# Where the last modulation blocks are accumulated, and when the first pair's second down weights are loaded

## The chip, the core and the metric

The kernel runs on one core of one Trainium2 chip. The metric is the device time of one execution in microseconds (us). The engines named below are TensorE (PE), VectorE (DVE), ScalarE (ACT), GpSimd (POOL) and SyncE (SP, which here only issues DMAs and waits).

## What is computed

One decoder layer on 512 tokens of width 1024, all in float32:

```python
ada = (silu(c) @ w_ada + b_ada).reshape(1, 6, 1024)      # six vectors
shift1, scale1, gate1, shift2, scale2, gate2 = ada
h = x * (1.0 + scale1) + shift1
q, k, v, cb, cc, cx = split(h @ w_in)                    # each 512 wide
attn = stick_breaking_attention(q, k, v)                 # 8 heads of 64
conv = cb * causal_depthwise_conv(cc * cx, conv_w)       # width 3
mix  = concatenate([attn, conv]) @ w_out
x  = layer_norm(ALPHA * x + gate1 * mix, ln1_g, ln1_b)
h2 = x * (1.0 + scale2) + shift2
moe = hierarchical_moe(h2)   # 32 experts, 2 of 8 in the best of 4 groups per token
x  = layer_norm(ALPHA * x + gate2 * moe, ln2_g, ln2_b)
```

Stick-breaking attention takes sigmoids of the scores, multiplies `1 - sigmoid` along the keys from behind (a scan), and multiplies that with the sigmoid of the score itself. An expert is `(silu(h @ w_gate) * (h @ w_up)) @ w_down`, with 3 x 1 MB of weights.

## The kernel before

Every engine's program is written out by hand, in one fixed order, with semaphores between the engines. SP carries nearly all the loads in one queue of instructions: a wait in it holds back all loads behind it.

**Stages.** (1) `shift1` and `scale1` and the first projections, as `x` and `w_in` arrive. (2) The rest of `w_in` in nine blocks of 1 MB (`w_stage`, two buffers) and the other four vectors of `ada` in sixteen blocks of 1 MB (`ada_stage`, three buffers, blocks 8 to 23). VectorE does a block in `ada(i)`: nine dependent instructions (lines 775, 777 seven times, 779) into `acc_rows`. Three buffers mean that the load of block i waits for `ada(i-3)`. (3) Four pairs of heads. (4) Output projection, norm, modulation, routing. (5) The experts, two at a time. (6) The second norm and the output.

**Stage 3, pair p.** PE (from line 1240 on) does `scores(p)` (line 1206), `attend(p-1)` (line 1237), and then `conv_proj(3p)`, `turn_probs(2p)`, `conv_proj(3p+1)`, `turn_probs(2p+1)`, `conv_proj(3p+2)`. `conv_proj(n)` (line 1226, eight matmuls) is one 128-column block of the convolution's three inputs, in the order cc, cc, cx, cx, cb, cb and the same again; it writes one PSUM bank and so waits until product n-1 has been read from it (`conv_ev`). `turn_probs(h)` (line 1215, ten transposes) waits for the probabilities of head h (`prob_done`). ScalarE takes the sigmoids, GpSimd masks them (lines 487 and 490), and VectorE does `weights_of(h)`: the scan (line 825) as soon as `stay` is masked, and the product (line 829) once `prob` is masked too. `conv(n)` on VectorE reads product n: nothing for cc (ScalarE copies it out), line 840 and three more instructions for cx, line 848 for cb. In pair 0 only `conv(2)` has work, in pair 1 `conv(3)`, `conv(4)` and `conv(5)`, in pair 2 `conv(8)`, in pair 3 `conv(9)`, `conv(10)` and `conv(11)`.

VectorE's loop over the pairs ends with what `ada_in_pair` lists: blocks 20 and 21 in pair 0, 22 in pair 1, 23 in pair 2, none in pair 3. Blocks 8 to 19 come before the loop.

**From stage 3 to 4.** SP waits for all of `ada` (line 368), then issues four small router loads (lines 369 to 372) and `wo`, the 4 MB of `w_out` (line 373), into space that `ada_stage` also used. PE does `attend(3)`, spreads rows 0 to 3 of `acc_rows` over the partitions (`spread_row`, line 1259), waits for `wo` (`ld_wo`) and starts `project_out(0)` (line 1273). `row_done` counts the spread rows: the rows 4 and 5 follow `project_out(0)`, the rows 6 and 7 come behind `route(2)`. ScalarE's queue issues the loads of `g1r` and `b1r`, 512 KB each (lines 654 and 655), behind the copy of `attend(3)`'s result.

**Expert weights.** A ring of three pairs, `w_gu[u][e]` and `w_dn[u][e]`: pair u, expert e, three 1 MB loads each. SP first waits for `row_done` 6. The space of `w_dn[0][1]` is the end of `acc_rows`, so its load (`load_dn(0, 1, HALF)`) also waits for `row_done` 8. Pair 1 waits for `av_done` 4 and `conv_ev` 12 (the end of stage 3), pair 2 for `out_done` 8 (all of the output projection), and its second expert for `logit_done` 4 and the stores of `h2`. From then on `refill` loads the next pair into what the last one freed: first the gate and up weights of pair 3 once `gu_done` is 1, that is once the first expert's matmuls (line 1347) are over. PE gets the first tokens by an indirect gather (`xg`, line 520), which waits for the slot table that VectorE and PE work out behind `route(3)`.

Of the kernel before, what the change touches and what calls it, by code (L numbers as in the profile page):

```python
# [46 lines left out]
HALF = NE // 2  # L47
# [45 lines left out]
def layer_kernel(nc, x, c, w_ada, b_ada, w_in, conv_w, w_out, ln1_g, ln1_b, w_router_group,  # L93
# [3 lines left out]
    with ctx:  # L97
# [6 lines left out]
        def sem(name):  # L104
            return ctx.enter_context(nc.semaphore(name))
# [148 lines left out]
        row_done, row_ev, rows_ready, scaled = sem("row_done"), sem("row_ev"), sem("rows_ready"), sem("scaled")  # L254
# [21 lines left out]
        def acc_of(i):  # L276
            return acc_rows[:, w_cols(i - ADA1)]
# [18 lines left out]
        def landed(eng, what):  # L296

            buf, ld, before_it = stage_of(what)
            eng.wait_ge(ld, 16 * (before_it + 1))
            return buf  # L300
# [23 lines left out]
        def _(sp):  # L324
# [31 lines left out]
            for what in SEQ:  # L356
                kind, i = what
# [17 lines left out]
            def load_gu(u, e, ex):  # L375
                for g, w in enumerate((w_gate, w_up)):
                    src = w[0, bass.ds(ex, 1)].rearrange("o (p k) f -> p (o k) f", k=KC)
                    sp.dma_start(w_gu[u][e][:, g], src).then_inc(ld_gu[u][e], 16)  # L378

            def load_dn(u, e, ex):  # L380
                src = w_down[0, bass.ds(ex, 1)].rearrange("o (a p) n -> p (o a) n", p=P)
                sp.dma_start(w_dn[u][e][:], src).then_inc(ld_dn[u][e], 16)  # L382
# [3 lines left out]
            for j in range(RING):  # L386
                if j == 1:
                    sp.wait_ge(av_done, NH // 2)
                    sp.wait_ge(conv_ev, len(CONV_OUT))
                if j == 2:  # L390
                    sp.wait_ge(out_done, 2 * TC)
                for e in range(2):
                    if (j, e) == (2, 1):
                        sp.wait_ge(logit_done, TC)
                        for n in range(2):
                            sp.wait_ge(st_h2[n], 32)
                    load_gu(j, e, j + e * HALF)
                    if (j, e) == (0, 1):
                        sp.wait_ge(row_done, 8)
                    load_dn(j, e, j + e * HALF)  # L400

            def refill(i, u, first=False):

# [346 lines left out]
        def _(dve):  # L750
# [3 lines left out]
            def did(ins):  # L754
                count[0] += 1
                ins.then_inc(dve_did, 1)

            def settle():

                dve.wait_ge(dve_did, count[0])  # L760

            def link(ins):
                did(ins)
                settle()
# [6 lines left out]
            def ada(i):  # L771

                st = landed(dve, ("ada", i))
                acc = acc_of(i)
                link(w.tensor_scalar(acc, st[:, 0], csil[:, 3, 0:1], None, ALU.mult))
                for k in range(1, KC):
                    link(w.scalar_tensor_tensor(out=acc, in0=st[:, k], scalar=csil[:, 3, k:k + 1], in1=acc,  # L777
                                                op0=ALU.mult, op1=ALU.add))
                w.scalar_tensor_tensor(out=acc, in0=b24[:], scalar=ident[:, i:i + 1], in1=acc,
                                       op0=ALU.mult, op1=ALU.add).then_inc(ada_done, 1)  # L780
# [35 lines left out]
            dve.wait_ge(consts, 1)  # L816
            for i in range(ADA1, 20):
                ada(i)
            ada_in_pair = {0: (20, 21), 1: (22,), 2: (23,), 3: ()}

            def weights_of(h):

                st = stay[h % 2]
                dve.wait_ge(stay_masked, 2 * h + 2)
                w.tensor_tensor_scan(out=st[:, 0:ZW][:, ::-1], data0=st[:, 0:ZW][:, ::-1], data1=block_end[:, ::-1],  # L825
                                     initial=1.0, op0=ALU.mult, op1=ALU.max).then_inc(scan_done, 1)
                dve.wait_ge(scan_done, h + 1)
                dve.wait_ge(take_masked, 2 * h + 2)
                w.tensor_tensor(prob[h % 2][:], prob[h % 2][:], st[:, 1:ZW + 1], ALU.mult).then_inc(prob_done, 1)

            def conv(n):
                kind, f = CONV_OUT[n]
                y, u = cc_sb[f % 2], u_conv
                if kind == "cc":
                    return
                dve.wait_ge(conv_done, n + 1)
                dve.wait_ge(conv_ev, n)
                settle()
                if kind == "cx":
                    w.tensor_tensor(u[:], ps[:, 6], y[:], ALU.mult).then_inc(conv_ev, 1)  # L840
                    dve.wait_ge(conv_ev, n + 1)
                    link(w.tensor_scalar(y[:], u[:], cwT[:, 2 * NF + f:2 * NF + f + 1], None, ALU.mult))
                    link(w.scalar_tensor_tensor(out=y[:, 1:], in0=u[:, :T - 1], scalar=cwT[:, NF + f:NF + f + 1],
                                                in1=y[:, 1:], op0=ALU.mult, op1=ALU.add))
                    did(w.scalar_tensor_tensor(out=y[:, 2:], in0=u[:, :T - 2], scalar=cwT[:, f:f + 1],
                                               in1=y[:, 2:], op0=ALU.mult, op1=ALU.add))
                else:
                    w.tensor_tensor(mixT[:, NF + f], ps[:, 6], y[:], ALU.mult).then_inc(conv_ev, 1)

            dve.wait_ge(consts, 8)  # L850
            for p in range(NPH):
                weights_of(2 * p)
                conv(3 * p)
                weights_of(2 * p + 1)
                conv(3 * p + 1)
                conv(3 * p + 2)
                for i in ada_in_pair[p]:
                    ada(i)


            dve.wait_ge(row_ev, 6)
# [249 lines left out]
            i = TC - 1  # L1111
# [341 lines left out]
```

## Time and profile before

| | us |
|---|---|
| median of 3 runs | 607.32 (606.79 to 608.8) |
| profiled execution, own time | 606.77 |
| profiled execution, span | 605.0 |
| PE busy | 492.3 (81%) |
| VectorE busy | 284.1 (47%) |
| DMA, over the span | 164.11 MB, mean 271 GB/s |

Times in the rows are counted from the span's start. Between the span and the execution's own time lie 1.8 us that no row shows. The page cuts the span into 40 slices of 15.1 us. Its chain of the work that ended last is PE to 54%, SP's queue to 15%, DMA to 12% and VectorE to 11% of the span. An entry such as "[4.93 <-DVE prob L829]" says that the engine stood idle for 4.93 us before that row, and that what ended the wait was line 829 on VectorE.

### The profile page before, as it was taken

How to read it: one execution, taken by the hardware profiler on the slowest of the kernel's cores; microseconds unless marked ns; L12 is line 12 of the kernel's file. 1: busy time of each engine (PE TensorE's matmuls, PEld its weight loads, DVE VectorE, ACT ScalarE, POOL GpSimd, SP SyncE). 2: the span in 40 equal slices, each digit the busy share in tenths (PEclk: the TensorE clock that was granted, in tenths of full speed). 3: DMA queues.
4: the chain of work that ended last, by engine and by line, in shares of the span. 5: the costliest groups of instructions: out<-in, count | busy, mean ns of one | idle time of the engine just before them, and what ended most of it. 6: DMA issues, size and time to landing. Idle time of an engine off the chain costs nothing.

```text
span 605.0 us, 6476 instructions
## 1 busy us (share of the span) xinstructions
PE 492.3 (81%) x2426; PEld 263.9 (44%) x2426; DVE 284.1 (47%) x481; ACT 99.8 (16%) x161; POOL 125.8 (21%) x117
## 2 busy tenths in 40 slices
PE   2999999996999999999813999999979778887100
PEld 1545478443544444445512555555534434444000
DVE  4566999529481920785376132232321121122395
ACT  1000210413141411011221111211111111010010
POOL 2000000603060400455542012111111111000076
PEclk9999999999999999999855999999998988899755
DMA  8998789505022341730199999999999999996433
GB/s 296 355 363 255 254 281 311 179 1 195 14 69 71 94 195 70 284 133 35 64 421 414 385 385 415 414 416 417 417 418 416 419 418 417 417 419 282 157 150 134
DMA packets 66723, 164.11 MB, mean 271 GB/s; under 512 B 7768, under 2 KB 43660, under 8 KB 58508
## 3 DMA queue, kind: packets, MB, share of 16 engines
q1 hardware_dynamic: 60992, 152.22, 66.0%
q0 software_dynamic: 4608, 8.40, 3.7%
q10 hardware_dynamic: 1100, 3.19, 1.3%
q8 instruction: 14, 0.23, 0.2%
q14 instruction: 9, 0.07, 0.0%
HBM read 159.59 MB, written 12.58 MB: 285 GB/s over the span
## 4 chain that ended last, share of the span: by engine, by line
PE 54%; SPq 15%; DMA 12%; DVE 11%; POOL 3%; issue 2%; ACT 1%; POOLq 1%; DVEq 0%
SPq L378 10%; PE ps L1226 10%; PE ps L1347 9%; DMA w_gu<-in_w_up_dram 8%; PE ps L1149 7%; PE ps L1273 7%; PE ps L1196 5%; SPq L382 4%; PE ps L1356 4%; PE ps L1189 2%; DVE acc_rows L777 2%; PE ps L1215 2%; PE ps L1259 1%; DMA xs<-in_x_dram 1%; PE ps L1340 1%
## 5 line engine op out<-in xcount | busy, mean ns | idle before, releaser
L1347 PE MATMUL ps<-w_gu,xT 128*64 128x256 f32 x1024 | 126.4, 403 | 24.8 <-DMA w_gu<-in_w_up_dram 21.7
L1347 PEld LDWEIGHTS ps<-w_gu,xT 128*64 128x64 f32 x1024 | 75.4, 144 | 66.3 <-DMA w_gu<-in_w_up_dram 17.2
L1226 PE MATMUL ps<-hT,w_stage 128*128 128x512 f32 x192 | 85.7, 600 | 0.0
L1049 DVE TENSOR_TENSOR hid<-ps,silu_sb 128x128 f32<-128x128 f32 x32 | 9.3, 292 | 127.7 <-ACT silu_sb L704 113.8
L1057 DVE TENSOR_TENSOR ysb<-ps,rows_gate 64x512 f32<-64x512 f32 x64 | 44.0, 688 | 51.9 <-PE ps L1356 51.4
L1356 PE MATMUL ps<-w_dn,hidT 128*64 128x512 f32 x256 | 61.3, 599 | 0.6 <-ACT hidT L698 0.4
L526 POOL DMA_INDIRECT y_dram<-ysb,slot_row x16 | 16.1, 1005 | 202.2 <-DVE ysb L1057 202.2
L777 DVE SCALAR_TENSOR_TENSOR acc_rows<-ada_stage,csil,acc_rows 128x256 f32<-128x256 f32 x112 | 55.3, 494 | 4.0
L1273 PE MATMUL ps<-wo,mixT 128*128 128x512 f32 x128 | 55.6, 592 | 0.0
L1226 PEld LDWEIGHTS ps<-hT,w_stage 128*128 128x128 f32 x192 | 36.0, 192 | 41.6 <-issue 41.6
L1149 PE MATMUL ps<-hT,w_first 128*128 128x512 f32 x96 | 45.1, 618 | 0.9 <-DVE hT L803 0.9
L1273 PEld LDWEIGHTS ps<-wo,mixT 128*128 128x128 f32 x128 | 24.2, 190 | 29.6 <-issue 29.6
L704 ACT ACTIVATE silu_sb<-ps 128x128 f32<-128x128 f32 x32 | 8.9, 277 | 139.7 <-PE ps L1347 136.4
L487 POOL TENSOR_SCALAR_AFFINE_SELECT stay<-stay 128x384 f32<-128x384 f32 x8 | 5.3, 660 | 127.7 <-ACT stay L618 127.7
L1196 PE MATMUL ps<-w_stage,hT 128*128 128x256 f32 x128 | 27.8, 379 | 0.0
L1356 PEld LDWEIGHTS ps<-w_dn,hidT 128*64 128x64 f32 x256 | 17.1, 136 | 24.0 <-issue 20.9
L1149 PEld LDWEIGHTS ps<-hT,w_first 128*128 128x128 f32 x96 | 18.3, 199 | 20.2 <-issue 20.2
L825 DVE TENSOR_TENSOR_SCAN stay<-stay,block_end 128x1280 f32<-128x1280 f32 x8 | 23.8, 2975 | 5.5 <-POOL stay L490 5.5
L1196 PEld LDWEIGHTS ps<-w_stage,hT 128*128 128x128 f32 x128 | 24.3, 190 | 3.7 <-issue 0.5
L1340 PE MATMUL ps<-ident,xg 128*128 128x128 f32 x128 | 18.4, 289 | 9.3 <-DMA xg<-h_dram,slot_tok 9.3
L789 DVE SCALAR_TENSOR_TENSOR acc_cols<-ada_in,csil,acc_cols 128x512 f32<-128x512 f32 x28 | 21.1, 752 | 1.2 <-DMA ada_in<-in_w_ada_dram 0.2
L1340 PEld LDWEIGHTS ps<-ident,xg 128*128 128x128 f32 x128 | 14.4, 146 | 15.2 <-DMA xg<-h_dram,slot_tok 9.4
(184 smaller groups left out, 479.2 us busy)
## 6 DMA issues: line engine op xcount, KB each, us to landing
w_gu<-in_w_gate_dram SPq DMA_DIRECT2D x32, 1024.0 KB, 19.2
w_gu<-in_w_up_dram SPq DMA_DIRECT2D x32, 1024.0 KB, 23.3
w_dn<-in_w_down_dram SPq DMA_DIRECT2D x32, 1024.0 KB, 24.5
ada_stage<-in_w_ada_dram SPq DMA_DIRECT2D x16, 1024.0 KB, 7.2
w_stage<-in_w_in_dram SPq DMA_DIRECT2D x9, 1024.0 KB, 9.6
ada_in<-in_w_ada_dram SPq DMA_DIRECT2D x16, 512.0 KB, 9.7
wo<-in_w_out_dram SPq DMA_DIRECT2D x1, 4096.0 KB, 14.4
y_tok<-y_dram SPq DMA_DIRECT2D x8, 512.0 KB, 7.4
```

The costliest lines, as they stand in the source:

```text
L378: sp.dma_start(w_gu[u][e][:, g], src).then_inc(ld_gu[u][e], 16)
L382: sp.dma_start(w_dn[u][e][:], src).then_inc(ld_dn[u][e], 16)
L777: link(w.scalar_tensor_tensor(out=acc, in0=st[:, k], scalar=csil[:, 3, k:k + 1], in1=acc, op0=ALU.mult, op1=ALU.add))
L825: w.tensor_tensor_scan(out=st[:, 0:ZW][:, ::-1], data0=st[:, 0:ZW][:, ::-1], data1=block_end[:, ::-1], initial=1.0, op0=ALU.mult, op1=ALU. ...
L1057: ins = w.tensor_tensor(ysb[u][e * HD:(e + 1) * HD, b * 512:(b + 1) * 512], ps[b * HD:(b + 1) * HD, 6 + e, :], gate2r[b * HD:(b + 1) * HD, ...
L1149: ins = t.matmul(ps[:, n], w_first[:, k, n * P:(n + 1) * P], hT[:, k], start=k == 0, stop=k == KC - 1)
L1196: ins = t.matmul(dst[:, 0:CW], hT[:, k, i * P:(i + 1) * P], st[:, k], start=k == 0, stop=k == KC - 1)
L1226: ins = t.matmul(ps[:, 6], st[:, k, (f % 2) * P:(f % 2 + 1) * P], hT[:, k], start=k == 0, stop=k == KC - 1)
L1273: ins = t.matmul(ps[:, 4 + 2 * (i % 2) + n], mixT[:, k, i * P:(i + 1) * P], wo[:, k, n * 512:(n + 1) * 512], start=k == 0, stop=k == KC - 1)
L1340: ins = t.transpose(flat[:, k * P:(k + 1) * P], xg[u][:, k * P:(k + 1) * P], ident[:])
L1347: ins = t.matmul(ps[a * SLOTS:(a + 1) * SLOTS, 2 + e, 0:2 * P], xT[u][:, k, e * SLOTS:(e + 1) * SLOTS], w_gu[slot][e][:, :, k, a * P:(a + ...
L1356: ins = t.matmul(ps[b * SLOTS:(b + 1) * SLOTS, 6 + e, :], hidT[e][:, a * SLOTS:(a + 1) * SLOTS], w_dn[slot][e][:, a, b * 512:(b + 1) * 512 ...
```

## The change

Two edits. On VectorE each pair now does one block of `ada`, 20 + p, right behind `weights_of(2p + 1)` and ahead of `conv(3p + 1)`. On SP the load of the first pair's second down weights, with its wait for `row_done` 8, moves from the end of pair 0 to behind pair 1 and the wait for `out_done`.

```diff
@@ SP @@
                 if j == 2:
                     sp.wait_ge(out_done, 2 * TC)
+                    sp.wait_ge(row_done, 8)
+                    load_dn(0, 1, HALF)
                 for e in range(2):
...
                     load_gu(j, e, j + e * HALF)
-                    if (j, e) == (0, 1):
-                        sp.wait_ge(row_done, 8)
-                    load_dn(j, e, j + e * HALF)
+                    if (j, e) != (0, 1):
+                        load_dn(j, e, j + e * HALF)
@@ VectorE @@
             for i in range(ADA1, 20):
                 ada(i)
-            ada_in_pair = {0: (20, 21), 1: (22,), 2: (23,), 3: ()}
...
                 weights_of(2 * p + 1)
+                ada(20 + p)
                 conv(3 * p + 1)
                 conv(3 * p + 2)
-                for i in ada_in_pair[p]:
-                    ada(i)
```

VectorE, the last pair, from the end of pair 2 on. Names: `stay` and `prob` with the head's buffer number, `cc_sb` the convolution's buffer, `ada_stage` the block, `ps` the PSUM. Before:

```order
L775 TENSOR_SCALAR acc_rows_66<-ada_stage0_63,csil_139 128x256
L777 SCALAR_TENSOR_TENSOR acc_rows_66<-ada_stage0_63,csil_139,acc_rows_66 128x256 x7
L779 SCALAR_TENSOR_TENSOR acc_rows_66<-b24_87,ident_121,acc_rows_66 128x256
L825 SCALAR_TENSOR_TENSOR stay0_68<-stay0_68,block_end_70 128x1280
L829 TENSOR_TENSOR prob0_89<-prob0_89,stay0_68 128x1280
L840 TENSOR_TENSOR u_conv_86<-ps,cc_sb1_92 128x512
L842 TENSOR_SCALAR cc_sb1_92<-u_conv_86,cwT_138 128x512
L843 SCALAR_TENSOR_TENSOR cc_sb1_92<-u_conv_86,cwT_138,cc_sb1_92 128x511
L845 SCALAR_TENSOR_TENSOR cc_sb1_92<-u_conv_86,cwT_138,cc_sb1_92 128x510
L825 SCALAR_TENSOR_TENSOR stay1_69<-stay1_69,block_end_70 128x1280
L829 TENSOR_TENSOR prob1_90<-prob1_90,stay1_69 128x1280
L848 TENSOR_TENSOR mixT_106<-ps,cc_sb0_91 128x512
```

And now, from the first scan of the last pair on:

```order
L825 SCALAR_TENSOR_TENSOR stay0_68<-stay0_68,block_end_70 128x1280
L829 TENSOR_TENSOR prob0_89<-prob0_89,stay0_68 128x1280
L840 TENSOR_TENSOR u_conv_86<-ps,cc_sb1_92 128x512
L842 TENSOR_SCALAR cc_sb1_92<-u_conv_86,cwT_138 128x512
L843 SCALAR_TENSOR_TENSOR cc_sb1_92<-u_conv_86,cwT_138,cc_sb1_92 128x511
L845 SCALAR_TENSOR_TENSOR cc_sb1_92<-u_conv_86,cwT_138,cc_sb1_92 128x510
L825 SCALAR_TENSOR_TENSOR stay1_69<-stay1_69,block_end_70 128x1280
L829 TENSOR_TENSOR prob1_90<-prob1_90,stay1_69 128x1280
L776 TENSOR_SCALAR acc_rows_66<-ada_stage0_63,csil_139 128x256
L778 SCALAR_TENSOR_TENSOR acc_rows_66<-ada_stage0_63,csil_139,acc_rows_66 128x256 x7
L780 SCALAR_TENSOR_TENSOR acc_rows_66<-b24_87,ident_121,acc_rows_66 128x256
L848 TENSOR_TENSOR mixT_106<-ps,cc_sb0_91 128x512
```

Block 23 (three rows with `acc_rows`) has gone from ahead of the last pair's first scan to between its last product and the first line 848; pair 1 has the same new order with block 21.

SP's queue, from the first pair's second expert to the third pair (`w_gu01` is pair 0, expert 1). Before:

```order
L378 DMA w_gu01_50<-in_w_gate_dram 128x2048
L378 DMA w_gu01_50<-in_w_up_dram 128x2048
L382 DMA w_dn01_56<-in_w_down_dram 128x2x1024 [waits row_done]
L378 DMA w_gu10_51<-in_w_gate_dram 128x2048 [waits conv_ev,av_done]
L378 DMA w_gu10_51<-in_w_up_dram 128x2048
L382 DMA w_dn10_57<-in_w_down_dram 128x2x1024
L378 DMA w_gu11_52<-in_w_gate_dram 128x2048
L378 DMA w_gu11_52<-in_w_up_dram 128x2048
L382 DMA w_dn11_58<-in_w_down_dram 128x2x1024
```

And now:

```order
L378 DMA w_gu01_50<-in_w_gate_dram 128x2048
L378 DMA w_gu01_50<-in_w_up_dram 128x2048
L378 DMA w_gu10_51<-in_w_gate_dram 128x2048 [waits conv_ev,av_done]
L378 DMA w_gu10_51<-in_w_up_dram 128x2048
L382 DMA w_dn10_57<-in_w_down_dram 128x2x1024
L378 DMA w_gu11_52<-in_w_gate_dram 128x2048
L378 DMA w_gu11_52<-in_w_up_dram 128x2048
L382 DMA w_dn11_58<-in_w_down_dram 128x2x1024
L382 DMA w_dn01_56<-in_w_down_dram 128x2x1024 [waits row_done,out_done]
```

The load of `w_dn01`, with the wait for `row_done`, stands behind the six loads of pair 1.

## Rows read from the trace of the kernel before

**Rows 1.** Page, part 2: what the DMA engines moved, in 40 slices of 15.1 us.

```profile
GB/s 296 355 363 255 254 281 311 179 1 195 14 69 71 94 195 70 284 133 35 64 421 414 385 385 415 414 416 417 417 418 416 419 418 417 417 419 282 157 150 134
```

**Rows 2.** Chain that ended last, 296 to 345 us: start us, us, what.

```profile
319.86 7.50 DMA xg<-h_dram,slot_tok
```

**Rows 3.** Busy time by stretch: length, engines, PEclk, DMA share, GB/s.

```profile
151.00:152.00 1.00, 1.00 (x6) 1.00 (x5) 0.93 (x3) 0.00 (x0) 0.00 (x0) 0.50 0.62 197
335.00:338.00 3.00, 2.52 (x29) 1.47 (x27) 1.02 (x6) 0.54 (x2) 0.00 (x0) 1.00 0.83 269
```

**Rows 4.** PE in time, attention stage: start us, us, line, idle before and releaser.

```profile
138.00 7.13 PE L1226 MATMUL ps<-hT,w_stage 128*128 128x512 f32 x16
150.06 2.16 PE L1215 MATMUL ps<-ident,prob 128*128 128x128 f32 x10 [4.93 <-DVE prob L829]
152.02 7.91 PE L1226 MATMUL ps<-hT,w_stage 128*128 128x512 f32 x16
...
160.85 7.05 PE L1226 MATMUL ps<-hT,w_stage 128*128 128x512 f32 x16
...
207.85 1.31 PE L1215 MATMUL ps<-ident,prob 128*128 128x128 f32 x10 [0.57 <-DVE prob L829]
...
216.96 7.05 PE L1226 MATMUL ps<-hT,w_stage 128*128 128x512 f32 x16
...
229.78 13.90 PE L1273 MATMUL ps<-wo,mixT 128*128 128x512 f32 x32
```

**Rows 5.** VectorE in time, the same stage and the same columns.

```profile
97.95 0.35 DVE L775 TENSOR_SCALAR acc_rows<-ada_stage,csil 128x256 f32<-128x256 f32 x1
...
102.39 0.35 DVE L775 TENSOR_SCALAR acc_rows<-ada_stage,csil 128x256 f32<-128x256 f32 x1
...
112.01 2.82 DVE L825 TENSOR_TENSOR_SCAN stay<-stay,block_end 128x1280 f32<-128x1280 f32 x1 [5.10 <-POOL stay L490]
115.49 1.72 DVE L829 TENSOR_TENSOR prob<-prob,stay 128x1280 f32<-128x1280 f32 x1 [0.66 <-POOL prob L490]
...
133.45 0.69 DVE L840 TENSOR_TENSOR u_conv<-ps,cc_sb 128x512 f32<-128x512 f32 x1 [11.24 <-PE ps L1226]
...
149.93 0.68 DVE L840 TENSOR_TENSOR u_conv<-ps,cc_sb 128x512 f32<-128x512 f32 x1
...
152.62 2.82 DVE L825 TENSOR_TENSOR_SCAN stay<-stay,block_end 128x1280 f32<-128x1280 f32 x1
155.48 1.49 DVE L829 TENSOR_TENSOR prob<-prob,stay 128x1280 f32<-128x1280 f32 x1
```

**Rows 6.** GpSimd in time: the last mask of the third head's `stay`.

```profile
137.87 0.47 POOL L490 TENSOR_SCALAR_AFFINE_SELECT stay<-stay 128x128 f32<-128x128 f32 x1
```

**Rows 7.** PE in time, expert stage: two waits for weights.

```profile
454.15 5.34 PE L1347 MATMUL ps<-w_gu,xT 128*64 128x256 f32 x32 [2.79 <-DMA w_gu<-in_w_up_dram]
...
479.59 3.67 PE L1347 MATMUL ps<-w_gu,xT 128*64 128x256 f32 x32 [2.24 <-DMA w_gu<-in_w_up_dram]
```

**Rows 8.** SP queue in time: start us, us, issues.

```profile
203.24 0.55 SPq L369 DMA_DIRECT2D w_r<-in_w_router_group_dram  x1
...
205.72 0.43 SPq L373 DMA_DIRECT2D wo<-in_w_out_dram  x1
...
299.73 0.38 SPq L382 DMA_DIRECT2D w_dn<-in_w_down_dram  x1
```

**Rows 9.** ScalarE queue in time: first of the two norm loads.

```profile
226.37 0.35 ACTq L654 DMA_DIRECT2D g1r<-in_ln_g_dram  x1
```

**Rows 10.** DMA issues, KB each, median us to landing.

```profile
wo<-in_w_out_dram SPq DMA_DIRECT2D x1, 4096.0 KB, 14.4
...
g1r<-in_ln_g_dram ACTq DMA_DIRECT2D x1, 512.0 KB, 4.0
b1r<-in_ln_b_dram ACTq DMA_DIRECT2D x1, 512.0 KB, 5.0
```

**Rows 11.** Line 526 alone, window 562 to 566 us: landing time of the last scatter.

```profile
DMA to landing us min/median/max: 3.6/3.6/3.6
```

## The prediction

> **What bounds the kernel now.** I read the page's row of what the DMA engines moved first [rows 1]. From slice 20 to slice 35 (302 to 545 us) it stands at 385 to 421 GB/s and hardly moves: the expert stage is bound by its transfers. Before that (slices 16 to 19, 242 to 302 us) the engines are mostly idle, and PE sets the time, with gaps. So a microsecond won ahead of 302 us counts only as far as it brings the saturated stretch forward, and what brings that forward is to be read at its start.
>
> At that start the ring of six experts is being filled. SP has stood at the wait for `row_done` 8 until 299.73 us [rows 8], and then issues 13 loads of 1 MB, 13.6 MB, which at some 416 GB/s take 33 us, to about 335 us with their latency. The first refill can be issued when the first expert's gate and up matmuls are over, near 336 us. The stretch 335 to 338 us, the only dip there, still has the DMA engines 83% busy [rows 3]. The end of the filling and the first refill thus meet: neither hides much of the other. PE's start on the experts hangs on the gather of the first tokens: issued at 319.86 us, landed 7.50 us later, among those loads [rows 2].
>
> In the attention stage I look at PE in time for gaps [rows 4]: 4.93 us before 150.06 us, for a product of VectorE, and 0.57 us before 207.85 us, for another. VectorE shows why [rows 5]: it had blocks 20 and 21 to do ahead of pair 1's first scan, while earlier it had waited 11.24 us for PE ahead of 133.45 us. After the 4.93 us PE's clock is at 0.50 [rows 3], which is the lower level, 1.2 GHz.
>
> **Edit one, block by block.** A block takes 102.39 - 97.95 = 4.44 us [rows 5].
>
> Block 20 moves into the 11.24 us in which VectorE waited: nothing, as long as that cover is longer than 4.44 us.
>
> Block 21 leaves the front of pair 1. The mask of `stay` ends at 137.87 + 0.47 = 138.3 us [rows 6]. Scan and product, with GpSimd's masks between, take 115.49 + 1.72 - 112.01 = 5.2 us when nothing is ahead of them [rows 5], so the product is there at 143.6 us. PE ends `conv_proj(3)` at 138.00 + 7.13 = 145.1 us [rows 4] and no longer waits. Turning, projecting and turning again took 216.96 - 207.85 = 9.1 us at full clock and 160.85 - 150.06 = 10.8 us behind the gap, so 1.7 us of clock go too. PE is ready for `conv_proj(5)` at 154.2 us instead of 160.85: 6.6 us won.
>
> But that product needs its bank, and the bank is read by `conv(4)`, which now stands behind block 21. Line 840 starts at 145.2 us, its four instructions take 152.62 - 149.93 = 2.7 us, scan and product 155.48 + 1.49 - 152.62 = 4.35 us [rows 5]: 152.2 us. The block adds 4.44, the read 0.7: 157.4 us. So PE waits 3.2 us anew, behind ten short transposes, and 3.4 us of the 6.6 are left.
>
> Does the clock fall again there? Of two waits for weights in the expert stage, the one of 2.79 us is followed by matmuls that take 5.34 us, the one of 2.24 us by the same in 3.67 us [rows 7]. 3.2 us lies on the side of the fall, and the price is 5.34 - 3.67 = 1.7 us, the same as behind the 4.93. I take the fall: net 3.4 - 1.7 = 1.7 us won by the end of pair 1. The bounds are 0 and 1.7.
>
> Block 22 goes from pair 1's end into pair 2, ahead of `conv(8)`, where VectorE waits for PE as it did in pair 0: nothing. Block 23 leaves the front of pair 3, where PE waited 0.57 us [rows 4]; PE is there at 207.3 us less the 1.7. But it comes to stand ahead of `conv(10)`. From 207.3 us VectorE needs 2.7 + 4.35 + 4.44 = 11.5 us, to 218.8, less the 1.7: **block 23 ends at 217.1 us**, in the old order it ended ahead of 203.24 us, when SP went on [rows 8]. `conv(10)` ends at 217.8 us, while PE was ready at 207.3 + 9.1 - 1.7 = 214.7 us: 3.1 us of waiting, and likely 1.7 us of clock. PE has spread its rows at 229.78 - 216.96 + 217.8 + 1.7 = 232.3 us.
>
> What is queued behind block 23 is what costs. SP waits for it with five loads, `wo` the last. From the first to `wo` it took 205.72 - 203.24 = 2.5 us [rows 8], and `wo` lands 14.4 us after its issue [rows 10]: 217.1 + 2.5 + 14.4 = 234.0 us. Until now it landed at 220.1 us, 9.7 us ahead of its use, and that cover is gone. Moreover, ScalarE's two loads of 512 KB were issued at 226.37 us [rows 9], with `wo` long landed. Now they come near 229 us, into its flow. Nothing in the trace shows those three together, so the bounds are 0 and 1.05 MB / 416 GB/s = 2.5 us. I take 2.5: the gather of [rows 2] among loads took 7.5 us, while a scatter of no more bytes in quiet took 3.6 us [rows 11], so transfers of different queues do share. `project_out(0)` starts at 236.5 instead of 229.78 us: **6.7 us later**. PE has waited 4.2 us then, so one more fall of the clock, 1.7 us (bounds 0 and 1.7): **8.4 us**.
>
> The Trainium skill ("DMA: Bandwidth & Descriptors", section on queues, rings and completion order) says that each DMA engine goes round the queues that have work, a packet at a time. By that rule the two norm loads take their full bytes out of `wo`'s flow, and the stretch is at its upper end, against this change; with an order by arrival it would be 0 and the sum 2.5 us smaller. The rows of gather and scatter speak for the rule, no row shows it for `wo`.
>
> Behind `project_out(0)` nothing on PE's and VectorE's way to routing changes, and there is no slack between them: rows 4 and 5, the norm and three more products follow one another. The 8.4 us arrive whole at the gather's issue.
>
> **Edit two.** SP issues the six loads of pair 1 directly behind pair 0, near 256 us, into engines that are idle. That is 6.3 MB, 15.1 us at 416 GB/s, off what is left at `row_done` 8. The remaining 7.3 MB take 17.6 us and have landed about when the gather is issued. This doesn't bring the end forward by 15 us, since the first refill must still wait for the first expert; the DMA engines stand idle in between. What it gives is a gather in quiet: 3.6 us in place of 7.5, **3.9 us** sooner, bounds 0 and 3.9. That passes on: gather, transposes, first expert, first refill, and then 26 experts at an unchanged rate. Nothing waits behind the moved `row_done` 8 that could have gone earlier, but for pair 2's first expert, which waited there before as well. The stores of `h2` (two of them) now run among loads; nobody waits for these two closely.
>
> For the gather, the same page's section on the anatomy of one DMA gives 2.0 us plus bytes / 436 GB/s, an estimate of 3.2 us for 512 KB in quiet. By that the sum would be 0.4 us smaller.
>
> **Sum.** +6.7 +1.7 -3.9 = +4.5 us. The profiled execution took 606.77 us, span and the 1.8 us around it, and would become 611.3; it lies 0.55 us under the median of three. The median would be 607.32 + 4.5 = **611.8 us**.
>
> **Rivals.**
> A. The clock holds through the 3.2 us of pair 1. All from there is 1.7 us earlier, block 23 too: 610.1 us. For it: the 2.24 us that cost nothing. Against: 2.79 us that did, and the transposes ahead of the wait.
> B. `wo` isn't stretched by the norm loads: 2.5 us less, 609.3 us. Against it speaks the gather's 7.5 us.
> C. More than one of these, say the clock holds both in pair 1 and ahead of `project_out(0)`: 3.4 us less, 608.4 us, no difference that can be told.
> D. Faster: the filling of the ring is the bound, not the gather. If the refills could follow the last filling load at once, the 6.3 MB loaded early would shorten the saturated stretch by 15.1 us, and with +8.4 the time would be 600.6 us. It decides if the first expert's matmuls are over when the 7.3 MB have landed, near 320 us on the old scale. That the gather is issued only at 319.86 us [rows 2] speaks against it.
> E. Edit two gives nothing: the gather takes its 7.5 us even so (its cost lies elsewhere, or the loads of pair 2 still run). Then 607.32 + 8.4 = 615.7 us.
>
> **How the numbers follow.** Forecast 0.44, A 0.22, B 0.08, C 0.13, D 0.07, E 0.06. A measurement of this kernel tells about 0.3%, 1.8 us, from no change. Slower by more: forecast, A, E and half of B, 0.76. Within: C and half of B, 0.17. Faster: D, 0.07. The range 607.3 to 613.9 leaves out D, E and the edges: C down to no loss at all, and the forecast with a wait or a clock stretch some 2 us larger.
>
> **What would show it.** Right: no wait ahead of pair 1's first turning; waits near 3 us for line 848 ahead of `conv_proj(5)` and `conv_proj(11)`; PE waiting some 4 us for the load of `wo`, landed 16 to 17 us after its issue; DMA moving over 380 GB/s for some 27 us from 256 us on; an idle hole in it ahead of the first refill; the first gather in under 4.5 us. Wrong: `wo` landed ahead of PE's need, which would take 6 to 8 us from the sum, or a saturated stretch that starts by more than 5 us sooner against the gather's issue.

## The result, and the profile after

| | median us | single runs |
|---|---|---|
| before | 607.06 | 606.59 to 608.8 |
| the change | 614.15 | 612.26 to 614.85 |

The ratio is 1.0107, with a 95% interval of 1.0076 to 1.0137: slower, by 7.1 us where 4.5 were forecast. The ratio times the 607.32 us of the forecast is 613.8 us, at the very end of the range 607.3 to 613.9; the raw median, 614.15, lies 0.25 us outside it. Run again on other chips, the same kernel gave 609.97 us beside 607.44 (ratio 1.0047, 1.0029 to 1.0065, 12 runs) and 610.53 beside 606.96 (1.0073, 1.0044 to 1.0101, 7 runs). The three profiled executions of it have spans of 612.5, 610.8 and 609.2 us, against 605.0 before.

Lines of `kernel.py` differ by one or two between the versions (`conv_proj` is 1226 before and 1225 here, `project_out` 1273 and 1272). PE in time (start us, us, line, idle before and releaser), the attention stage and what follows, of the changed kernel; it answers to [rows 4]:

```profile
138.96 7.13 PE L1225 MATMUL ps<-hT,w_stage 128*128 128x512 f32 x16
145.93 1.26 PE L1214 MATMUL ps<-ident,prob 128*128 128x128 f32 x10
...
158.36 8.80 PE L1225 MATMUL ps<-hT,w_stage 128*128 128x512 f32 x16 [3.19 <-DVE mixT L848]
...
218.80 7.10 PE L1225 MATMUL ps<-hT,w_stage 128*128 128x512 f32 x16 [3.19 <-DVE mixT L848]
...
238.97 16.57 PE L1272 MATMUL ps<-wo,mixT 128*128 128x512 f32 x32 [7.13 <-DMA wo<-in_w_out_dram]
255.38 1.88 PE L1258 MATMUL ps<-acc_rows,ones 128*128 128x512 f32 x4
...
335.59 1.97 PE L1339 MATMUL ps<-ident,xg 128*128 128x128 f32 x8 [5.60 <-DMA xg<-h_dram,slot_tok]
```

This execution is 1.0 us late before anything that the change moves: `scores(0)` starts at 108.24 us and not at 107.28. Take that off every time here. The 4.93 us ahead of 150.06 us [rows 4] are gone: `turn_probs(2)` starts at 145.93 us, right behind `conv_proj(3)`. Two new waits of 3.19 us stand for line 848, at 158.36 and at 218.80 us. The first is followed by a product of 8.80 us (clock lost), the second by one of 7.10 (none lost). Then PE waits 7.13 us for `wo`, and the first product of the output projection takes 16.57 us instead of 13.90 [rows 4].

VectorE in time shows who holds back line 848; it answers to [rows 5]:

```profile
151.69 1.49 DVE L829 TENSOR_TENSOR prob<-prob,stay 128x1280 f32<-128x1280 f32 x1
153.09 0.35 DVE L776 TENSOR_SCALAR acc_rows<-ada_stage,csil 128x256 f32<-128x256 f32 x1
...
157.53 0.68 DVE L848 TENSOR_TENSOR mixT<-ps,cc_sb 128x512 f32<-128x512 f32 x1
...
213.54 0.35 DVE L776 TENSOR_SCALAR acc_rows<-ada_stage,csil 128x256 f32<-128x256 f32 x1
...
217.97 0.68 DVE L848 TENSOR_TENSOR mixT<-ps,cc_sb 128x512 f32<-128x512 f32 x1
```

The probabilities' product (line 829) ends at 153.1 us; the block goes from 153.09 to 157.53 us, and only then is the bank read. In pair 3 the block runs from 213.54 to 217.97 us.

SP's queue and the DMA issues (KB each, median us to landing), which answer to [rows 8, 10]:

```profile
218.08 0.55 SPq L369 DMA_DIRECT2D w_r<-in_w_router_group_dram  x1
...
220.56 0.43 SPq L373 DMA_DIRECT2D wo<-in_w_out_dram  x1
...
344.58 0.33 SPq L378 DMA_DIRECT2D w_gu<-in_w_gate_dram  x1
```

```profile
wo<-in_w_out_dram SPq DMA_DIRECT2D x1, 4096.0 KB, 18.4
...
g1r<-in_ln_g_dram ACTq DMA_DIRECT2D x1, 512.0 KB, 7.9
b1r<-in_ln_b_dram ACTq DMA_DIRECT2D x1, 512.0 KB, 10.1
```

`wo` goes out at 220.56 us, 14.8 us later than before, and takes 18.4 us and not 14.4; the two norm loads take twice as long as before. The first refill goes out at 344.58 us, 8.3 us later than before:

```profile
336.25 0.33 SPq L378 DMA_DIRECT2D w_gu<-in_w_gate_dram  x1
```

The chain of waits (start us, us, what) has the first gather, as in [rows 2], and the page's row answers to [rows 1] (slices of 15.3 us here):

```profile
331.74 3.81 DMA xg<-h_dram,slot_tok
```

```profile
GB/s 296 355 362 236 253 273 318 173 137 70 2 67 70 1 179 176 41 412 370 34 261 292 190 402 419 417 417 417 416 418 417 418 418 417 417 418 302 152 150 137
```

The gather takes 3.81 us, not 7.50. Slices 17 and 18 carry 412 and 370 GB/s where 133 and 35 stood: pair 0's five loads, which come 12 us later than before, and the six early loads of pair 1. Slice 22 (337 to 352 us) has 190: the hole ahead of the first refill.

### The profile page after: what moved, and what is told of

It is laid out like the page before. It is cut to its first block, busy times and chain, and to the rows that moved or that the text cites. A ratio compares the mean times of both kernels' runs of the same rounds, so it can differ in the third digit from the quotient of the medians.

```text
span 612.5 us, 6477 instructions
## 1 busy us (share of the span) xinstructions
PE 497.7 (81%) x2426; PEld 265.7 (43%) x2426; DVE 283.0 (46%) x481; ACT 99.9 (16%) x161; POOL 126.7 (21%) x117
## 3 DMA queue, kind: packets, MB, share of 16 engines
q10 hardware_dynamic: 1100, 3.19, 1.3%
## 4 chain that ended last, share of the span: by engine, by line
PE 32%; SPq 15%; DMA 13%; DVE 8%; POOL 2%; issue 2%; ACT 1%; POOLq 1%; DVEq 0%
SPq L378 10%; PE ps L1346 9%; DMA w_gu<-in_w_up_dram 8%; PE ps L1272 7%; PE ps L1225 6%; SPq L382 4%; PE ps L1355 4%; DMA wo<-in_w_out_dram 3%; PE ps L1339 1%; PE ps L1288 1%; POOL xs L574 1%; DVE xs L1100 1%; POOL rstd L507 1%; PE ps L1205 1%; PE ps L1258 1%
## 5 line engine op out<-in xcount | busy, mean ns | idle before, releaser
L1346 PE MATMUL ps<-w_gu,xT 128*64 128x256 f32 x1024 | 128.2, 407 | 22.6 <-DMA w_gu<-in_w_up_dram 19.4
L1346 PEld LDWEIGHTS ps<-w_gu,xT 128*64 128x64 f32 x1024 | 76.7, 146 | 64.6 <-issue 16.8
L1272 PE MATMUL ps<-wo,mixT 128*128 128x512 f32 x128 | 58.3, 615 | 7.1 <-DMA wo<-in_w_out_dram 7.1
L1339 PE MATMUL ps<-ident,xg 128*128 128x128 f32 x128 | 18.4, 289 | 5.6 <-DMA xg<-h_dram,slot_tok 5.6
L692 ACT COPY xT<-ps 128x1024 f32<-128x1024 f32 x16 | 16.2, 1012 | 24.2 <-PE ps L1339 24.2
## 6 DMA issues: line engine op xcount, KB each, us to landing
wo<-in_w_out_dram SPq DMA_DIRECT2D x1, 4096.0 KB, 18.4
```

The costliest lines, as they stand in the source:

```text
L1272: ins = t.matmul(ps[:, 4 + 2 * (i % 2) + n], mixT[:, k, i * P:(i + 1) * P], wo[:, k, n * 512:(n + 1) * 512], start=k == 0, stop=k == KC - 1)
L1339: ins = t.transpose(flat[:, k * P:(k + 1) * P], xg[u][:, k * P:(k + 1) * P], ident[:])
L1346: ins = t.matmul(ps[a * SLOTS:(a + 1) * SLOTS, 2 + e, 0:2 * P], xT[u][:, k, e * SLOTS:(e + 1) * SLOTS], w_gu[slot][e][:, :, k, a * P:(a + ...
```

## Experiments

A time is the median of the runs; the kernel before, run beside them, gave 607.38 us (with the blocks alone, the load alone, two blocks in each of two pairs, and the first run with the norm loads held back), 607.44 (with pair 1 or pair 3 free, the old load order, and the change again) and 606.96 (with `wo` held, and the last two).

### The blocks alone

```diff
@@ the changed kernel, SP @@
                 if j == 2:
                     sp.wait_ge(out_done, 2 * TC)
-                    sp.wait_ge(row_done, 8)
-                    load_dn(0, 1, HALF)
...
-                    if (j, e) != (0, 1):
-                        load_dn(j, e, j + e * HALF)
+                    if (j, e) == (0, 1):
+                        sp.wait_ge(row_done, 8)
+                    load_dn(j, e, j + e * HALF)
```

> Only the new places of the four blocks; the load of the first pair's second down weights stays at the end of pair 0. My theory: all of the loss is here. In the changed kernel the start of the output projection moved by 8.2 us (238.97 - 229.78, less the 1.0 us that the profiled run was late before the attention stage) and its first product took 2.7 us more at the lower clock, and the quiet gather gave 3.7 back. Without that gift: 607.1 + 8.2 + 2.7 = 618 us, and the first gather takes about 7.5 us again. Rival, the earlier loads give nothing (their gain is an accident of the comparison): 614 us, as with both edits.

617.0 us (611.7 to 618.9), ratio 1.0141 (1.0094 to 1.0188). The rival's 614 lies inside its interval as well, so the time alone doesn't part them; the trace does. PE in time:

```profile
158.97 8.80 PE L1224 MATMUL ps<-hT,w_stage 128*128 128x512 f32 x16 [3.18 <-DVE mixT L847]
...
219.41 7.11 PE L1224 MATMUL ps<-hT,w_stage 128*128 128x512 f32 x16 [3.18 <-DVE mixT L847]
...
238.88 15.41 PE L1271 MATMUL ps<-wo,mixT 128*128 128x512 f32 x32 [6.43 <-DMA wo<-in_w_out_dram]
...
340.00 1.97 PE L1338 MATMUL ps<-ident,xg 128*128 128x128 f32 x8 [9.83 <-DMA xg<-h_dram,slot_tok]
```

And the chain:

```profile
331.92 8.03 DMA xg<-h_dram,slot_tok
```

The wait for `wo` is 6.43 us, and the gather again takes 8.03 us.

### The load alone

```diff
@@ the kernel before, SP @@
                 if j == 2:
                     sp.wait_ge(out_done, 2 * TC)
+                    sp.wait_ge(row_done, 8)
+                    load_dn(0, 1, HALF)
...
-                    if (j, e) == (0, 1):
-                        sp.wait_ge(row_done, 8)
-                    load_dn(j, e, j + e * HALF)
+                    if (j, e) != (0, 1):
+                        load_dn(j, e, j + e * HALF)
```

> Only the new place of the load; the blocks stay in the loop's old places. My theory: the gather gets quiet engines and lands in about 3.8 instead of 7.5 us, nothing else moves: 607.1 - 3.7 = 603.4 us. Rival D of the prediction, the filling of the ring is the bound: 607.1 - 15.1 = 592 us. Rival E, the early loads give nothing: 607.1 us.

602.98 us, ratio 0.9927 (0.9905 to 0.995): 4.4 us faster. The chain:

```profile
319.52 3.95 DMA xg<-h_dram,slot_tok
```

The gather goes out when it did before, and takes 3.95 us. So edit two is a gain of some 4 us by itself. The 6.3 MB of pair 1, loaded some 50 us earlier, are not worth their 15 us (rival D), and not nothing (rival E).

### Two blocks in pair 0, two in pair 2

```diff
@@ the changed kernel, VectorE @@
                 weights_of(2 * p + 1)
-                ada(20 + p)
+                for i in ((20, 21), (), (22, 23), ())[p]:
+                    ada(i)
                 conv(3 * p + 1)
```

> Both edits, but blocks 20 and 21 behind the second head of pair 0, and 22 and 23 behind the second head of pair 2, where VectorE waited 11.2 and 12.5 us for PE and two blocks take 8.9. My theory: no wait in pair 1 (6.6 us won), none ahead of pair 3 (0.8 won), no new wait for a product's bank, w_out landed long before its use, quiet gather (3.7 won): 607.1 - 11.1 = 596 us. Rival, the blocks find no real cover (they slow PE's or GpSimd's work beside them, or w_out's 4 MB delay the last projection weights): 600 us or more, with a wait in pair 1 or 3.

596.24 us (594.97 to 597.82), ratio 0.9815 (0.9791 to 0.9838): 11.1 us faster than before, which is the forecast of this run to 0.3 us. The gap in pair 0 is in [rows 5]; the one that takes blocks 22 and 23 is this, of VectorE before the change:

```profile
195.59 0.69 DVE L840 TENSOR_TENSOR u_conv<-ps,cc_sb 128x512 f32<-128x512 f32 x1 [12.45 <-PE ps L1226]
```

PE in time, of this run:

```profile
144.62 1.25 PE L1215 MATMUL ps<-ident,prob 128*128 128x128 f32 x10
...
153.69 7.05 PE L1226 MATMUL ps<-hT,w_stage 128*128 128x512 f32 x16
...
209.03 7.05 PE L1226 MATMUL ps<-hT,w_stage 128*128 128x512 f32 x16
...
221.86 13.90 PE L1273 MATMUL ps<-wo,mixT 128*128 128x512 f32 x32
```

None of these rows has a wait in brackets any more, neither for the turning nor for line 848 nor for `wo`.

### The same blocks, the old order of the loads

The diff of this run is that of the last one, made to the kernel with the blocks alone.

> Blocks as in the run with two in pair 0 and two in pair 2, but the old order of the expert loads. My theory: the two gains are independent, 7.4 us by the blocks alone: 607.1 - 7.4 = 599.7 us, the first gather takes 7.5 us. Rival, the ring's filling now matters more, since PE comes sooner to the experts but not the filling: still about 600, but the first experts wait for their weights.

600.73 us, ratio 0.9895 (0.9865 to 0.9924). The gather:

```profile
314.41 7.42 DMA xg<-h_dram,slot_tok
```

With the new load order it was 4.5 us fewer (on another chip), and with the old blocks 4.4: with blocks that cost nothing, the gain of the load stays the same.

### Pair 1 without a block

```diff
-                ada(20 + p)
+                for i in ((20, 21), (), (22,), (23,))[p]:
+                    ada(i)
```

> Both edits, but block 21 goes to pair 0, so that pair 1 has none; 22 and 23 stay where the change put them. It takes away the wait in pair 1 alone. My theory: 3.2 us of waiting and 1.7 us of clock fewer, and all behind it, block 23 and w_out too, earlier by as much: 614.1 - 4.9 = 609.2 us. PE still waits some 3 us for line 848 in pair 3 and some 7 us for w_out. Rival, the wait in pair 1 costs nothing since w_out's landing sets the time whatever PE does: 614 us.

604.13 us (10 runs), ratio 0.9952 (0.9935 to 0.997). Beside it the change had 609.97, so 5.8 us fewer, where 4.9 were expected; but my absolute number, taken from the first median of 614.1, missed by 5 us, and one detail fell. PE in time, and PE's weight loads:

```profile
212.47 10.04 PE L1226 MATMUL ps<-hT,w_stage 128*128 128x512 f32 x16 [3.19 <-DVE mixT L848]
...
228.34 14.00 PE L1273 MATMUL ps<-wo,mixT 128*128 128x512 f32 x32
```

```profile
228.34 0.30 PEld L1273 LDWEIGHTS ps<-wo,mixT 128*128 128x128 f32 x2 [0.72 <-DMA wo<-in_w_out_dram]
```

The wait for line 848 is there (3.19 us). The wait for `wo` has shrunk to 0.72 us of a weight load, and the matmuls show none. The clock fell in pair 3 this time and the product took 10.04 us, so that PE and `wo` were ready at the same moment; `wo` took only 14.1 us here. The two costs hide each other: what PE loses ahead of `wo`'s landing costs nothing as long as `wo` is later still.

### Pair 3 without a block

```diff
-                ada(20 + p)
+                for i in ((20,), (21,), (22, 23), ())[p]:
+                    ada(i)
```

> Both edits, but block 23 goes to pair 2, so that pair 3 has none; 20 and 21 stay where the change put them. w_out's load then starts some 27 us sooner. My theory: what is left is pair 1's 1.7 us won net (3.4 if the clock holds), 0.8 us ahead of pair 3 and 3.7 us by the gather: 607.1 - 6.2 = 600.9 us (599.2 if the clock holds). Rival, the new place of block 23 costs only its own wait of 3.2 us, and the lateness of w_out would be found behind another wait: 614.1 - 3.2 = 610.9 us.

601.23 us, ratio 0.9899 (0.9874 to 0.9924). The rival is out by 9.7 us. PE in time:

```profile
157.63 8.80 PE L1226 MATMUL ps<-hT,w_stage 128*128 128x512 f32 x16 [3.19 <-DVE mixT L848]
...
227.54 13.90 PE L1273 MATMUL ps<-wo,mixT 128*128 128x512 f32 x32
```

Pair 1's wait and lost clock are as in the change, 3.19 and 8.80 us, and still the kernel is 6.2 us faster than before. Block 23's place decides the sign: 609.97 - 601.23 = 8.7 us by this one block.

### `wo` late, and nothing else

```diff
@@ two blocks in pair 0, two in pair 2; SP @@
             sp.wait_ge(ada_done, len(COLS) + NADACH - ADA1)
+            sp.wait_ge(conv_done, len(CONV_OUT) - 1)
             sp.dma_start(w_r[:, :, 0:NG], ...
```

> The kernel with two blocks in pair 0 and two in pair 2, with the router loads and w_out's load held until convolution product 10 is done. That puts w_out's issue 11 us ahead of PE's need, as in the changed kernel, with nothing else late: it prices the lateness alone. My theory: the load takes 17 to 18 us beside the norm loads, PE waits about 6 us for it and the first product of the output projection takes 2 to 3 us more at the lower clock: 596.2 + 8.5 = 604.7 us. Rival, the lateness is cheap by itself and the loss came from the waits in pairs 1 and 3: 596.2 + 2.7 (11.4 us to 14.1) at most = 598.9 us.

604.25 us (9 runs), ratio 0.9948 (0.9931 to 0.9964): 8.0 us over the 596.24. The DMA issue and PE in time:

```profile
wo<-in_w_out_dram SPq DMA_DIRECT2D x1, 4096.0 KB, 17.2
```

```profile
228.45 15.83 PE L1274 MATMUL ps<-wo,mixT 128*128 128x512 f32 x32 [5.92 <-DMA wo<-in_w_out_dram]
```

PE waits 5.92 us, and the product takes 15.83 and not 13.90 us. The ratios differ by 1.3%, which is the same 8 us. The four router loads are held along with `wo`, but the wait for `wo` is the only one of PE from here to the gather that the run with two and two does not have. One load that comes late costs 8 us by itself.

### The norm loads behind `wo`

```diff
@@ the changed kernel, ScalarE @@
+            act.wait_ge(ld_wo, 16)
             act.dma_start(g1r[:], ln1_g[0].partition_broadcast(P)).then_inc(ld_g1, 16)
```

> The changed kernel, with ScalarE's two norm loads held back until w_out has landed. w_out's load took 18.4 us there and 14.4 before. My theory: the 4.0 us are the two norm loads that share the DMA engines. It lands in 14.4 us again and the time falls by 4.0: about 610 us. Rival, the stretch has another cause (the small router loads ahead of it, the memory): still 18 us, 614 us.

609.17 us, ratio 1.0028 (0.9981 to 1.0075), with single runs at 606.5, 606.5, 611.8 and 612.4. `wo` took 13.8 us in its profile, so the rival, that the stretch has another cause, falls. But beside the 609.97 of the change on another chip the time tells nothing, so both were run again side by side, in more rounds:

> Again the changed kernel with the norm loads behind w_out's landing, beside the changed kernel on the same chip. My theory: w_out in 14 us and not 17 to 18, PE waits some 3 to 5 us less for it, and where the wait becomes short the clock is not lost at the first product: 4 to 6 us under the changed kernel. Rival, the difference of the two first comparisons (609.2 and 610.0 us) was real and the norm loads cost under 1 us.

> The changed kernel once more, as the partner of the run with the norm loads held back. My theory: between 610 and 614 us, the two medians so far, with single runs 5 us apart. Rival, one of the two medians so far was an accident and this one repeats the other within 1 us.

607.55 us (12 runs, 605.8 to 612.7), ratio 1.0016 (0.999 to 1.0042), and 610.53 us (7 runs, 609.9 to 615.9), ratio 1.0073 (1.0044 to 1.0101): 3.0 us between the medians, a little under the 4 to 6 that I expected, and well over the 1 us of the rival. For the change itself the other rival came true: 610.53 us repeats the 609.97 within 1 us, and the first median of 614.15 was not reached again. The change first, DMA issues and PE in time, then the run with the loads held back:

```profile
wo<-in_w_out_dram SPq DMA_DIRECT2D x1, 4096.0 KB, 16.5
...
g1r<-in_ln_g_dram ACTq DMA_DIRECT2D x1, 512.0 KB, 7.5
```

```profile
236.90 15.67 PE L1272 MATMUL ps<-wo,mixT 128*128 128x512 f32 x32 [3.52 <-DMA wo<-in_w_out_dram]
```

```profile
wo<-in_w_out_dram SPq DMA_DIRECT2D x1, 4096.0 KB, 14.2
...
g1r<-in_ln_g_dram ACTq DMA_DIRECT2D x1, 512.0 KB, 3.7
```

```profile
233.75 14.00 PE L1273 MATMUL ps<-wo,mixT 128*128 128x512 f32 x32 [1.28 <-DMA wo<-in_w_out_dram]
```

With the norm loads out of its way `wo` takes 14.2 us and not 16.5, and PE's wait shrinks to 1.28 us, behind which the clock holds: 14.00 against 15.67 us. Three executions of twelve lie near 612 us, and no profile caught one of these.

### The change again

> The changed kernel once more, in more rounds. My theory: 614 us, with single runs between 611 and 615, since the clock falls in some runs after the waits of 3.2 us and not in others (1.7 us each). Rival, a fixed time as the kernel before has: all runs within 1 us.

609.97 us (12 runs, 606.7 to 613.6). The rival falls: single runs spread over 7 us, where those of the kernel before beside them spread over 3.7 (which isn't the 1 us of the rival either). The expected 614 us fell too, by 4 us. A run at 606.7 us may be rival C, the clock held at more than one place; no profile caught it. This profile has the same two waits of 3.19 us, `wo` in 17.2 us, and a first product of 15.66. It is of an execution of 612.55 us, 2.6 us above the median of the twelve.

## Why the prediction was right, and where it was off

**What bounds it.** Confirmed. The filling of the ring wasn't the bound (rival D): the load alone gave 4.4 us, not 15. The signs that were named came: over 380 GB/s from 259 to 289 us (27 us were named), the hole ahead of the first refill, the gather in under 4.5 us.

**Block 21.** As worked out: turning without a wait, a new wait of 3.19 us (3.2 forecast), 1.7 us of clock (8.80 us for the product), and `scores(2)` 1.7 us sooner in the end (167.09 - 1.0 against 167.83). The clock fell there in all seven profiles that have this wait; rival A, that it holds, never came.

**Block 23.** It ended at 218.0 - 1.0 = 217.0 us (217.1 forecast), the wait was 3.19 us (3.1). The clock fell with it in four of seven profiles; I had counted on the fall for the moment at which PE is ready. In the first profile it held, so PE had spread its rows at 231.8 - 1.0 = 230.8 us and not at 232.3, and waited for `wo` the longer. This was of no weight for the time as long as `wo` was later still.

**The load of `wo`.** This is the term that was too small. Its issue was right (220.56 - 1.0 = 219.6). I gave it 14.4 + 2.5 = 16.9 us; it took 18.4, 17.2 and 16.5 us in the three profiles of the change, 17.7 with the blocks alone and 17.2 with nothing else late. The cause was the one named: with the norm loads held back it took 13.8 and 14.2. Rival B (no stretch) is out for the change. It came true only in the run without a block in pair 1, where the norm loads were issued 10.6 us behind `wo` and not 7.7 to 9.4: `wo` took 14.1 us there.

The stretch is 2.1 to 4.0 us, and not the 2.5 us that the bytes of the norm loads make at full rate. By the round of the queues that the Trainium skill tells of ("DMA: Bandwidth & Descriptors", section on queues, rings and completion order) 2.5 us would be the end of it; the trace goes with the rule in that they share, and beyond it in the size. The trace shows where the rest lies. The end of the flow, before the change and then with it (stretches of 1 us; length, PE busy, PEclk, DMA share, GB/s; `wo` lands at 220.1 and at 238.93 us):

```profile
218.00:219.00 1.00, 1.00 (x4) 1.00 0.74 295
219.00:220.00 1.00, 1.00 (x4) 1.00 0.07 29
```

```profile
236.00:237.00 1.00, 0.00 (x0) 0.50 0.25 98
237.00:238.00 1.00, 0.00 (x0) 0.50 0.06 25
238.00:239.00 1.00, 0.03 (x1) 0.50 0.02 8
```

Read in stretches of half a microsecond, the full flow ends 13.3 us behind `wo`'s issue before the change and 15.4 to 15.6 us behind it in the three profiles of the change: 2.1 to 2.3 us more, about what the bytes make. What differs is the thin rest between there and the landing, 1.1 us before, and 2.9, 1.7 and 0.9 us in the three. Why it is longer in some executions I can't say.

**The clock ahead of `project_out(0)`.** Forecast 1.7 us; 2.7, 1.8 and 1.8 in the three profiles, 1.9 with `wo` held. In the first profile PEclk was 0.50 from 234 us to past 243, and PE resumed at 238.97 (stretches of 1 us; length, PE busy, PEclk, DMA share, GB/s):

```profile
233.00:234.00 1.00, 0.00 (x0) 0.97 1.02 414
234.00:235.00 1.00, 0.00 (x0) 0.50 1.02 406
...
243.00:244.00 1.00, 1.00 (x2) 0.50 0.00 0
244.00:245.00 1.00, 1.00 (x3) 0.91 0.00 0
```

So it isn't a fixed price: the lower level lasted 5.2 us past the end of the wait here, and 3.4 us in the other two profiles, and about half of that is what the product lost.

**Edit two.** The gather took 3.7 to 4.1 us in the ten profiles with the early loads, where 3.6 was taken from the scatter (the second estimate, 3.2 us, was further off), and 7.4 to 8.0 among loads: 3.7 us won in the profile (3.9 forecast). Rival E is out.

**The sum.** Of the profile: `project_out(0)` 9.2 us later, of which 1.0 was there before and 8.2 are the change's (6.7 forecast); 2.7 by the clock (1.7); -3.7 by the gather (-3.9). That is 7.2 us against 4.5, plus the 1.0, and the first refill is 8.3 us late. The expert stage and the tail then gave 0.8 us back, so the span is 7.5 us longer; where they won it was not looked into. The same three terms, each profile's own start taken off, make 7.1 + 1.8 - 3.4 = 5.4 us in the second profile and 6.3 + 1.8 - 3.5 = 4.6 us in the third. The third is the one in which the clock fell in both pairs, as the forecast had it, and in which the norm loads came 9.4 us behind `wo`.

The sign, the places and the mechanism were right; two terms were too small for the first comparison, the stretch of `wo` and the fall of the clock. The forecast of 4.5 us lies between the three medians' differences of 7.1, 2.5 and 3.6 us, and no profile takes the smallest of these apart. The range held the first only at its edge: it let the stretch of `wo` stop at 2.5 us and the fall of the clock at 1.7, which I had called bounds and which were only an estimate from bytes and rows of other places. That the first comparison came to lie inside by 0.1 us, and not outside, is luck.

## What to carry to other kernels

A filler put in a gap costs what is queued behind it, on all queues: block 23 found a place on VectorE that looked as good as the others, and it was the last thing that SP waited for ahead of a 4 MB load, 8.7 us by one block (the wait and the clock in pair 3 included). Look for the gaps in which the engine truly waits for another (11 and 12 us here, ahead of `conv(2)` and `conv(8)`), and fill those with two blocks before spreading them evenly, one per turn: 596.2 us instead of 610 to 614. And two edits in one change are to be timed apart: here one was worth 4.4 us and the other cost 9.6.

## What the runs showed of the hardware

The clock of PE fell with each of seven waits of 3.2 us at one place of the program, and with four of seven such waits at another; waits of 0.84 and 1.28 us for `wo` cost nothing. The three of the second place that held the clock are the three executions that had started latest (`scores(0)` at 108.23 us or later; the four others at 108.08 or earlier); seven profiles don't make that a cause. Where it fell, the next product lost 1.5 to 1.8 us, once 3.0 (10.04 for 7.05 us), and 1.5 to 2.7 us behind waits of 3.5 to 7.1. In the case of 3.0 the level was down by 212 us, before the wait ended at 212.47. Here is the more common one, in the changed kernel: the wait ended at 158.36 us, and the level changed only after it (length, PE busy, PEclk, DMA share, GB/s).

```profile
158.00:159.00 1.00, 0.64 (x2) 0.92 0.00 0
159.00:160.00 1.00, 1.00 (x3) 0.50 0.00 0
...
163.00:164.00 1.00, 1.00 (x4) 1.00 0.00 0
```

Whether small loads stretch a 4 MB one went with how far behind it they were issued. The two norm loads stretched `wo` by 2.1 to 4.0 us when they were issued 7.7 to 9.4 us behind it (five profiles), and not at all at 10.6 us (one profile, 14.1 us). No run moved this distance alone. They themselves took 7.2 to 10.1 us in all six, against 3.7 to 5.3 alone.

The change has the wider spread: 7 us in 12 runs and 6 us in 7, against 3.7 us in 23 of the kernel before and 3 us (594.97 to 597.82) in the four of the version without waits. That the clock makes the spread was not shown, since only the profiled executions show it, and the kernel before also has a wait of 4.93 us with a fall behind it. The starts differ as well, by up to 1.9 us at `scores(0)` (106.93 to 108.86 us in the profiles), in a stretch that no kernel here changed.
